# Two hybrid encoder layers on one core: the query tiles of the latent attention are computed inside branch B

## The reference

```python
c_q = rmsnorm(q_lat, P['mla_q_norm'][l])
qa = (c_q @ P['w_mla_uq'][l]).reshape(b, t, H_A, A_NOPE + A_ROPE)          # branch A: queries, 384 -> 8 x (64 + 32)
qa_nope, qa_rope = qa[..., :A_NOPE], rope(qa[..., A_NOPE:], q_pos)
...
o_a = sweep(mla_attend, (qa_nope, qa_rope), (kv[..., :A_NOPE], krope_all, kv[..., A_NOPE:]), q_pos, k_pos)
o_b = sweep(sb_attend, (q_b.reshape(b, t, H_B, D_B),), (kb_all, vb_all), q_pos, k_pos)

def sb_attend(q_args, kv_args, q_pos, k_pos):                              # branch B
    z = jnp.einsum('bqhd,bkhd->bhqk', q, k).astype(jnp.float32) * D_B ** -0.5
    strict = k_pos[None, :] < q_pos[:, None]
    log_beta = jax.nn.log_sigmoid(z)
    log_keep = jnp.where(strict, jax.nn.log_sigmoid(-z), 0.0)
    log_stick = lax.cumsum(log_keep, axis=3, reverse=True) - log_keep
    a = jnp.where(strict, jnp.exp(log_beta + log_stick), 0.0)
    return jnp.einsum('bhqk,bkhd->bqhd', a, v.astype(jnp.float32)).astype(v.dtype)
```

## Time and profile before

| | |
|---|---|
| time, median of 3 runs | 3132.85 us (3127.67 to 3133.35) |
| span of the profiled execution | 3130.1 us; its own time is not given apart from the runs above |
| TensorE busy | 2995.5 us, 96% of the span |
| VectorE, ScalarE, GpSimd busy | 1464.2, 1004.5, 1064.3 us |
| share of TensorE in the chain that ended last | 89% |
| branch B on TensorE, first layer | 644.1 to 715.35 us |
| from there to the first eviction of a `kA` tile | 715.35 to 742.86 us |

### The profile page before, as it was taken

One profiled execution on the slowest core, in us unless ns is written; L12 is line 12 of the kernel. 1 busy time (PEld: TensorE's weight loads), 2 busy tenths in 40 slices (PEclk: granted clock), 3 DMA queues, 4 the chain that ended last, 5 costly groups with the idle time before them and its releaser, 6 DMA issues.

```text
span 3130.1 us, 53679 instructions
## 1 busy us (share of the span) xinstructions
PE 2995.5 (96%) x22966; PEld 2755.5 (88%) x22966; DVE 1464.2 (47%) x1645; ACT 1004.5 (32%) x1625; POOL 1064.3 (34%) x517
## 2 busy tenths in 40 slices
PE   8999979999999989999999999799999999899997
PEld 7999977956888989999899999679567889899997
DVE  4554232854345455552265541337543554555522
ACT  3222233363445242222232222332634442322221
POOL 3333333312232433334333343333032424333432
PEclk9999989999999999999999999899999999999998
DMA  4222253112121222222212222321121113122121
GB/s 152 90 84 69 93 134 106 58 47 68 42 68 58 89 102 81 94 72 75 109 68 92 82 74 77 111 102 61 34 70 50 65 61 127 68 81 94 68 84 66
DMA packets 44109, 252.44 MB, mean 81 GB/s; under 512 B 6161, under 2 KB 6257, under 8 KB 27953
## 3 DMA queue, kind: packets, MB, share of 16 engines
q1 hardware_dynamic: 38016, 232.63, 21.0%
q0 software_dynamic: 5840, 17.50, 2.2%
q10 hardware_dynamic: 96, 0.08, 0.0%
HBM read 234.33 MB, written 15.85 MB: 80 GB/s over the span
## 4 chain that ended last, share of the span: by engine, by line
PE 89%; DVE 4%; ACT 4%; issue 2%; DMA 0%; DVEq 0%; SPq 0%; ACTq 0%
PE PS L656 39%; PE PS L661 19%; PE PS L911 13%; PE PS L593 2%; PE PS L678 2%; PE PS L1092 1%; PE PS L773 1%; PE PS L880 1%; PE PS L1068 1%; PE PS L689 1%; PE PS L831 1%; PE PS L1032 1%; PE PS L1037 1%; DVE xT L1573 1%; PE PS L1028 1%
## 5 line engine op out<-in xcount | busy, mean ns | idle before, releaser
L431 POOL TENSOR_TENSOR ring_r<-ring,piece_h 128x1024 fp32r<-128x1024 f32 (+1 forms) x232 | 611.5, 2637 | 996.3 <-ACT piece_h L1167 996.3
L1167 ACT ACTIVATE piece_h<-ring 128x1024 fp32r<-128x1024 f32 (+1 forms) x232 | 266.8, 1152 | 1144.8 <-PE PS L661 1122.8
L431 POOL TENSOR_TENSOR ring_r<-ring,piece_m 128x1024 fp32r<-128x1024 f32 (+1 forms) x162 | 345.2, 2137 | 788.9 <-ACT piece_m L1167 788.5
L656 PE MATMUL PS<-uT_r,piece_h 128*128 128x272 f32 x2688 | 556.8, 289 | 2.6 <-DVE sq L1608 2.6
L656 PE MATMUL PS<-u_l,piece_h 128*128 128x272 f32 x2688 | 557.2, 288 | 0.0
L661 PE MATMUL PS<-uT_r,ring_r 128*128 128x272 f32 x3232 | 438.1, 288 | 0.0
L656 PEld LDWEIGHTS PS<-uT_r,piece_h 128*128 128x128 f32 x2688 | 421.8, 188 | 3.5 <-ACT piece_h L1167 3.5
L656 PEld LDWEIGHTS PS<-u_l,piece_h 128*128 128x128 f32 x2688 | 422.0, 188 | 0.0
L661 PEld LDWEIGHTS PS<-uT_r,ring_r 128*128 128x128 f32 x3232 | 417.5, 188 | 0.0
L656 PE MATMUL PS<-act_l,piece_h 128*128 128x272 f32 x1408 | 292.5, 290 | 0.0
L656 PE MATMUL PS<-act_h,piece_h 128*128 128x272 f32 x1408 | 291.8, 289 | 0.0
(11 more groups left out here) (251 smaller groups left out, 4488.1 us busy)
## 6 DMA issues: line engine op xcount, KB each, us to landing
ring<-in_w_up SPq DMA_DIRECT2D x88, 1024.0 KB, 4.8
ring<-in_w_dn SPq DMA_DIRECT2D x64, 704.0 KB, 4.2
ring<-in_w_mg SPq DMA_DIRECT2D x48, 768.0 KB, 4.3
ring<-in_w_in SPq DMA_DIRECT2D x22, 1024.0 KB, 4.7
ring<-in_w_out SPq DMA_DIRECT2D x8, 1024.0 KB, 5.2
x_spill<-xT SPq DMA_DIRECT2D x2, 2176.0 KB, 21.2
xT<-x_spill SPq DMA_DIRECT2D x2, 2176.0 KB, 8.8
ring<-in_w_vb SPq DMA_DIRECT2D x8, 512.0 KB, 4.4
```

The source lines that it names most:

```text
L431: nc.gpsimd.tensor_tensor(ring_r[:, ch[0] % NSLOT, at:at + n], w, hi, ALU.subtract).then_inc(S["w_low"], 1)
L656: mm(PS[:, 2 * u + b, 0:HALF], w, x[k][:, HALF * b:HALF * b + HALF], start=first and k == 0 and n == 0, stop=False)
L1167: A(buf[:, hs, 0:n], ring[:, ch % NSLOT, at:at + n], ACT.Copy).then_inc(S["w_high"], 1)
```

## The change

The four query tiles `uq0`..`uq3` leave their place behind branch B. Their 24 products for a layer (`queries`) are put in front of the scores of given steps of branch B, by the table QUERY_AT: three products make one half of one tile, in bank 5. VectorE copies each half out (`query`), between its own steps. To free bank 5, all values of branch B go to bank 4, so the values of a pair of heads wait until the pair before has been copied out, and ScalarE makes that copy at the head of its step, in front of the weights. At the end of branch B TensorE raises the tile counters by two for both units, in place of the four tiles. Behind branch B `qr0` now comes first, then `sample_values`, then `qs0`, `qr1`, `qs1`. The queries' place in memory (`qAn`) is exchanged with that of two softmax buffers of branch A, because branch B uses the old place.

```diff
+QUERY_AT = {1: 2, 2: 1, 4: 1, 5: 2, 6: 1, 8: 1, 9: 1, 10: 1, 12: 1, 13: 1, 14: 1, 16: 1, 17: 1, 18: 3, 19: 3, 20: 3}
+QUERY_DONE = {}
+for _v, _n in QUERY_AT.items():
+    if sum(n for v, n in QUERY_AT.items() if v <= _v) % 3 == 0:
+        QUERY_DONE[_v] = len(QUERY_DONE)
...
-                pe.wait_ge(S["lat_ready"], l * 7 + 3)
-                for i in range(8):
+                for i in range(4, 8):
                     w = chunk(l, ch + 16 + i // 4)
                     at = (i % 4) * KQ * P
                     tile(TILES[27 + i], [(w[:, at + k * P:at + k * P + P], ql[:, k, :]) for k in range(KQ)])
-                    if i == 0:
+                    if i == 4:
                         sample_values(l)
...
-                    if i == 0 and hp >= 2:
-                        pe.wait_ge(S["sb_out"], l * 5 + hp - 1)
+                    if i == 0 and hp >= 1:
+                        pe.wait_ge(S["sb_out"], l * 5 + hp)
...
-                        ins = mm(PS[64 * e:64 * e + 64, 4 + hp % 2, P * j:SEQ], VB[:, j, DH * h:DH * h + DH], stick_weights(u)[:, e, :],
+                        ins = mm(PS[64 * e:64 * e + 64, 4, P * j:SEQ], VB[:, j, DH * h:DH * h + DH], stick_weights(u)[:, e, :],
...
+                def queries(j):
+
+                    i, b, k = j // 6, j // 3 % 2, j % 3
+                    if j == 0:
+                        pe.wait_ge(S["lat_ready"], l * 7 + 3)
+                    if k == 0 and j:
+                        pe.wait_ge(S["query_out"], l * 8 + j // 3)
+                    w = chunk(l, CH_M + 16)[:, (i * KQ + k) * P:(i * KQ + k + 1) * P]
+                    ins = mm(PS[:, 5, 0:HALF], w, ql[:, k, HALF * b:HALF * b + HALF], start=k == 0, stop=k == KQ - 1)
+                    if k == KQ - 1:
+                        ins.then_inc(S["query_done"], 1)
...
                 for v in range(N_BU + 3):
+                    for _ in range(QUERY_AT.get(v, 0)):
+                        queries(at)
+                        at += 1
...
-                pe.wait_ge(S["sb_out"], l * 5 + 3)
+                pe.wait_ge(S["sb_out"], l * 5 + 4)
+                pe.wait_ge(S["query_out"], l * 8 + 8)
                 alone(pe)
+                for u in range(2):
+                    pe.sem_inc(done[u], 2)
+                    pe.sem_inc(vacated[u], 2)
...
                 for v in range(N_BU + 2):
+                    if v >= 7 and v % 4 == 3:
+                        out_pair((v - 7) // 4)
                     if v >= 2:
                         weights(v - 2)
                     if v < N_BU:
                         soft(v)
-                    if v >= 7 and v % 4 == 3:
-                        out_pair((v - 7) // 4)
...
+                def query(n):
+
+                    dve.wait_ge(S["query_done"], l * 8 + n + 1)
+                    V.tensor_copy(qAn[:, n // 2, HALF * (n % 2):HALF * (n % 2) + HALF], PS[:, 5, 0:HALF]).then_inc(S["query_out"], 1)
...
+                    if u + 1 in QUERY_DONE:
+                        query(QUERY_DONE[u + 1])
+                query(7)
                 dve.wait_ge(S["sb_out"], l * 5 + 5)
```

More of the change, by code:

```diff
@@ L99 @@
 MASK_W = [128, 256, 384, 512, W_S]
+QUERY_AT = {1: 2, 2: 1, 4: 1, 5: 2, 6: 1, 8: 1, 9: 1, 10: 1, 12: 1, 13: 1, 14: 1, 16: 1, 17: 1, 18: 3, 19: 3, 20: 3}
+assert sum(QUERY_AT.values()) == 8 * 3
+QUERY_DONE = {}
+for _v, _n in QUERY_AT.items():
+    if sum(n for v, n in QUERY_AT.items() if v <= _v) % 3 == 0:
+        QUERY_DONE[_v] = len(QUERY_DONE)
 ACC_AT = {1: 1024, 2: 1280, 4: 1664, 3: 2176}
@@ L234, in build @@
         qAr = region(20184, 2, TOK)
-        qAn = region(21272, 4, TOK)
-        probs = [region(14320, 2, 512), region(30280, 2, 512), region(31304, 2, 512)]
+        qAn = region(30280, 4, TOK)
+        probs = [region(14320, 2, 512), region(21272, 2, 512), region(22296, 2, 512)]
         probT = [region(15344, 2, 512), region(16368, 2, 512)]
@@ L246, in build @@
             for name, at in (("ident_b", 13184), ("sb_mask_b", 13312), ("chunk_mask_b", 27800)))
-        o_l = [region_r(f"o_l{b}", at, 4, TOK) for b, at in enumerate((21272, 7008, 4832))]
+        o_l = [region_r(f"o_l{b}", at, 4, TOK) for b, at in enumerate((30280, 7008, 4832))]
         o_h = [region_r(f"o_h{b}", at, 4, TOK) for b, at in enumerate((11360, 27928, 13536))]
@@ L263, in build @@
             "merge_ready", "merge_step", "gate_done", "gate_out", "br_done", "br_out", "x_saved", "x_back", "init_ready", "tab_ps", "tab_sb", "u_norm", "u_high",
-            "w_high", "w_low", "half_read", "gate_step", "v_step", "split", "split_c", "vw_turned", "rows_ki", "silu_done", "ropes_in", "masks_ready")}
+            "w_high", "w_low", "half_read", "gate_step", "v_step", "split", "split_c", "vw_turned", "rows_ki", "silu_done", "query_done", "query_out", "ropes_in", "masks_ready")}
         done = [sem("tile_done0"), sem("tile_done1")]
@@ L975, in values @@
                     pe.wait_ge(S["sb_a_ready"], nb + u + 4)
-                    if i == 0 and hp >= 2:
-                        pe.wait_ge(S["sb_out"], l * 5 + hp - 1)
+                    if i == 0 and hp >= 1:
+                        pe.wait_ge(S["sb_out"], l * 5 + hp)
                     for e in range(2):
                         h = 2 * hp + e
-                        ins = mm(PS[64 * e:64 * e + 64, 4 + hp % 2, P * j:SEQ], VB[:, j, DH * h:DH * h + DH], stick_weights(u)[:, e, :],
+                        ins = mm(PS[64 * e:64 * e + 64, 4, P * j:SEQ], VB[:, j, DH * h:DH * h + DH], stick_weights(u)[:, e, :],
                                  start=i == 0, stop=i == 3, skip_group_check=True)
                     ins.then_inc(S["sb_pv"], 1)
+                def queries(j):
[8 more added lines that the diff above has]
+                        ins.then_inc(S["query_done"], 1)
                 pe.wait_ge(S["root"], l * N_NORM + NORMS["kv"][0] + 2)
                 alone(pe)
+                at = 0
                 for v in range(N_BU + 3):
+                    for _ in range(QUERY_AT.get(v, 0)):
+                        queries(at)
+                        at += 1
                     if v < N_BU:
@@ L1348, in mixer @@
                 act.wait_ge(S["rows_out"], 16 * (l * 12 + 12))
[L1349 to L1353, removed]
+                act.wait_ge(S["sb_pv"], l * (N_BP + 1) + N_BP + 2)
+                A(qB[:, :, SEQ:TOK], PS[:, 4, 0:P].rearrange("p (a b) -> p a b", a=4), ACT.Copy).then_inc(S["sb_out"], 1)
                 for i in range(4):
@@ L1430, in out_pair @@
                     act.wait_ge(S["sb_pv"], npv + 4 * p + 5)
-                    A(qB[:, p, 0:SEQ], PS[:, 4 + p % 2, :], ACT.Copy).then_inc(S["sb_out"], 1)
+                    A(qB[:, p, 0:SEQ], PS[:, 4, :], ACT.Copy).then_inc(S["sb_out"], 1)
                 for v in range(N_BU + 2):
+                    if v >= 7 and v % 4 == 3:
+                        out_pair((v - 7) // 4)
                     if v >= 2:
```

## The result

The change takes 3146.53 us (median of 5 runs, 3144.06 to 3173.22) against 3128.63 for the kernel before beside it: 1.0066 times the time, 95% interval 1.0036 to 1.0095. It is slower, as forecast. One of the five runs of the change, that of 3173.22 us, had a clock of 0.95 even in the dense stretches; the ratio is one of means and would be 1.0049 without it, and since the first profile is of this run, all rows of after are from the change run a second time, in the first group of experiments. There it took 3145.87 against 3128.74 us, 1.0048 [1.0034, 1.0062]: 15.0 us, between 10.6 and 19.4, where 11.1 were forecast.

A forecast was written before the change was run, and what follows sets the result against it. TensorE, with 89% of the chain, was taken as the bound. Per layer 7.3 + 0.2 - 3.55 + 1.6 = 5.55 us, 11.1 us for two, on 3132.85 gives 3143.95, say 3144.0 us; range 3137.5 to 3149.

The forecast's parts named there:

- Products added in branch B: In branch B, 24 query products cost 13.6 us a layer, partly hidden in waits, so branch B grows by 7.3 us.
- The waits for the weights: In branch B, the scores' waits for ScalarE's weights, 6.56 us a layer, are filled by queries and remain nowhere but once.
- VectorE's copies and bank 4: In branch B, VectorE's eight query copies and three waits for bank 4 cost nothing; uncovered, 3.4 and 1.7 us a layer.
- The lead-in: In branch B, a query behind a step's values costs 0.19 us extra, at 13 places 2.5 us a layer.
- the rival without it: In branch B, query weights load beside the values ahead, 2.6 us less a layer, 3138.75 us in all; chance 0.16.
- Four semaphore increments: At the end of branch B, TensorE's increments add 0.2 us a layer, bounds 0 and 0.5.
- What follows branch B: Behind branch B, four tiles of 11 us go but a new wait comes, so 3.55 us a layer are kept.
- The new wait: Behind branch B, TensorE waits 7.2 us ahead of qr1, until VectorE ends the selection and empties qr0.
- The rival in which this wait does not come: Behind branch B, VectorE empties qr0 in time; 7.2 and 1.6 us leave each layer, 3126.35 us in all; chance 0.06.
- The clock behind that wait: Behind the wait ahead of qr1, TensorE's clock falls to half, costing 1.6 us a layer, bounds 0 and 3.2.

The follow-up runs named there:

- e2: The kernel before, with all branch B values in bank 4 and ScalarE's pair copy at the step's head, queries not moved; 3129.74 us, ratio 1.0002.
- e1: The change, but VectorE ends the selection of block 3 before it waits for the copy of the decoded tokens' values; 3126.13 us, ratio 0.9986.
- e6: e1, but the last three of the selection's eight operations stay behind the wait for the decoded values' copy; 3128.94 us, ratio 0.9997.
- e8: e1, but only the first of the selection's eight operations stays ahead of the wait for the decoded values' copy; 3144.37 us, ratio 1.0040.
- e4: e1, with the query products also moved behind the sums of the step before, ahead of the values; 3121.34 us, ratio 0.9976.
- e7: e1, but the last two of the selection's eight operations stay behind the wait for the decoded values' copy; 3124.22 us, ratio 0.9984.
- e9: e1, but only the first three of the selection's eight operations stay ahead of the wait for the decoded values' copy; 3134.46 us, ratio 1.0020.
- e3: The change, with query products behind the sums of the step before and ahead of the values; 3143.00 us, ratio 1.0042.
- e5: e4, with VectorE copying each half query tile ahead of its selection round, not behind it; 3117.31 us, ratio 0.9963.
- e10: e5, with TensorE's four semaphore increments ahead of its wait for the last weights, not behind it; 3117.26 us, ratio 0.9954.

## Why the prediction was right in its course and too low in its size

By the stretches a layer grew by 7.1 us, where 5.55 were forecast.

**Products added in branch B: right.** Branch B with the first tile grew by 7.81 us. 0.49 of them are the longer idle time ahead of that tile (1.17 less 0.68), so the products' part is 7.32 us, against 7.3. The waits for the weights went as forecast, down to one a layer. VectorE's copies and bank 4 cost nothing: in the change TensorE waits for VectorE nowhere in branch B, and e2 shows no wait for bank 4.

**The lead-in: it exists, so the rival without it falls.** A lone query takes 0.65 us behind the values and 0.55 behind the sums; with the queries moved there, and no wait for VectorE in their way, branch B is 2.37 us shorter, near the 2.5 that the forecast gave for the lead-ins at the 13 places behind values. About half of it is in the query itself and half in the later start of what follows the sums. The first load of 128 by 128 weights is not hidden behind products with 128 by 64 weights here, and it is behind products of its own shape. The Trainium skill, "TensorE: Matmul & The Clock Gate", Part 2, step-by-step, says that loads of weights are pulled ahead of products in flight when the row groups don't conflict or the load goes to the background buffer. The traces agree behind the sums (0.22 us ahead) and not behind the values (none). That the shape of the weights is the reason is a reading of these two places; no run changed the shape alone.

**Four semaphore increments: too low.** 0.49 us against 0.2, at the upper bound. They are small, but they run one behind another on a queue that has nothing else to do.

**What follows branch B: right.** The new wait is 7.38 us, forecast 7.2, in its place and for its reason: e1 takes it away by an order of VectorE's work, and the change becomes faster than before. The rival in which this wait does not come was false for this kernel, and e1 is that rival made true. It was to be 6.5 us faster than before; e1 was 2.6 us faster by medians. The half clock under its first tile, 1.7 us in both layers, makes up most of the difference.

**The clock behind that wait: the step that failed, in size alone.** I put +1.6 us, the price of one fall in the rows of before, where the half clock lasted 3.3 us. Here it lasted 5.5 us and cost 2.7 us in one layer and 2.6 in the other. The mechanism is as forecast and the value lies inside the bounds of 0 and 3.2, but the single row that I took as the typical case is at the low end: the eight restarts behind waits of 3.4 to 7.4 us lost 1.7 to 3.0 us. That row stands behind a wait of 2.1 us; whether so short a wait makes the price smaller, no run here shows. The Trainium skill, "TensorE: Matmul & The Clock Gate", Part 1, "What's actually happening", says that the window over which the activity is watched runs freely and is not reset by the kernel's start. By that, the price of a fall would also hang on the moment at which the work goes on. The two layers behind the same 3.37 us (1.7 and 3.0) agree with it; no run here shows the cause of the spread.

So of the 1.6 us a layer that the forecast lacks, the clock is 1.1, the increments 0.3 and the wait 0.2. What the timing has over the stretches (15.0 against 14.2 us for two layers) is within its interval.

## What to carry to other kernels

Work moved into the gaps of a stage is worth only what the engine can start earlier behind it. Here 11 us of products left the place behind branch B and lengthened branch B by 7.3; and VectorE, whose order nobody had needed to look at while the work hid it, made TensorE wait 7.4: before moving cover away, follow what it covers, and reorder that engine too (here that turned a loss of 0.48% into a gain of 0.14%, and three more edits of order made it 0.46%). A wait of 3.4 to 7.4 us on TensorE cost itself and a fall of the clock here; take for that the mean over several falls, not one row.

## What the runs showed that I had not expected

**VectorE's operations beside GpSimd's.** In the change the last four large operations of the selection take 1.46, 1.56, 1.63 and 1.36 us (the chain shows the first and last at 1.47 and 1.37). In e1, where they run earlier, the same four take 1.22, 0.75, 0.69 and 0.43. In the change GpSimd splits branch B's output at the same time, in e1 it has nothing to do then. GpSimd in the change:

```profile
729.99 2.82 POOL L516 CAST o_h<-arena 128x544 fp32r<-128x544 f32 x4 [82.11 <-ACT arena L1375]
732.78 7.17 POOL L519 TENSOR_TENSOR o_l<-arena,o_h 128x544 fp32r<-128x544 f32 x4
```

Of the same operations in e6, the last three ran beside GpSimd's casts and took 0.75, 0.94 and 0.67 us, where e1 has 0.75, 0.69 and 0.43; so it is mainly the operations with two inputs (L519) that slow them. The Trainium skill, "SBUF — State Buffer", "SBUF: two separate sides", says that GpSimd shares a pair of ports with those operations of VectorE that have two inputs in SBUF or use a mode of two ports, and that whichever starts first holds the pair to its end. Three of the four operations have two such inputs, and the change's trace fits: they start 1.58 to 1.74 us apart, while GpSimd's four take 1.79 us on average. It fits the casts less, which also read SBUF and slow VectorE by 0.25 us at most in e6; no run here shows why. So part of the wait of 7.4 us is made by the neighbour: 5.65 us for the whole end of the selection without it (e1), 8.87 beside it.

**A gap of 1.17 us.** The clock fell over the gap ahead of the first tile in some layers (both of e1 and e8, the first of e4, e6, e7 and e9) and not in others (both of the change, of e3 and of e5). It held over the 0.68 us of the kernel before and of e10 in both layers. What decides it was not found out.
